# Three more projections of a two-layer transformer block as seven block products each

## What is computed

```python
# even layer; h, hc are the normed tokens and context, (256, 1024) each
aq, ak, av, nq, nk, nv = split_cols(h @ w_in, (512,) * 6)        # the same for hc
# odd layer
cq, ckv, kr, rq, rk, rv, rg = split_cols(h @ w_in, (256, 128, 32, 256, 256, 512, 512))
r = rms_norm(retention(rq, rk, rv, ...)) * silu(rg)              # rg of the 256 tokens alone
```

## Time and profile before

| | before |
|---|---|
| median of 3 runs | 1845.21 us (1843.87 to 1847.04) |
| the profiled execution | 1846.67 us |
| its span, first to last instruction | 1844.9 us |
| TensorE matmul busy | 1601.1 us (87%) |
| VectorE busy | 700.1 us (38%) |
| ScalarE busy | 337.3 us (18%) |
| moved | 538.32 MB, mean 292 GB/s |
| mean granted TensorE clock | 0.955 |

### The profile page before, as it was taken

How to read it: one execution, slowest core, us unless ns; L and a number is a source line. 1 busy time by engine, 2 the same in 40 slices (tenths; PEclk the granted TensorE clock), 3 DMA queues, 4 the chain that set the end, 5 groups by cost and what they waited for, 6 DMA issues and landing times. The chain is left out here.

```text
span 1844.9 us, 23772 instructions
## 1 busy us (share of the span) xinstructions
PE 1601.1 (87%) x9876; PEld 860.6 (47%) x9876; DVE 700.1 (38%) x1473; ACT 337.3 (18%) x836; POOL 37.8 (2%) x40
## 2 busy tenths in 40 slices
PE   6999999999999999999989889899998665665665
PEld 3844684447884654333333233374655332232322
DVE  1267838766755853323223131330643111020202
ACT  2222227412002842000000000122431000000000
POOL 0000200000000000000000000000000000000000
PEclk9999999999999999999999999999999888788877
DMA  9312238874345032899999999921359999999997
GB/s 384 139 46 91 92 137 368 373 303 171 137 183 214 18 137 90 354 428 428 427 429 427 428 427 428 385 98 71 138 227 377 426 428 427 426 428 427 426 428 300
DMA packets 39966, 538.32 MB, mean 292 GB/s; under 512 B 4394, under 2 KB 4906, under 8 KB 6964
## 3 DMA queue, kind: packets, MB, share of 16 engines
q1 hardware_dynamic: 39860, 536.81, 70.2%
HBM read 535.74 MB, written 1.05 MB: 291 GB/s over the span
## 5 line engine op out<-in xcount | busy, mean ns | idle before, releaser
L675 PE MATMUL bank<-mem 128*32 128x256 f32 (+13 forms) x9112 | 1490.9, 473 | 221.3 <-DMA mem<-in_moe 145.5
L675 PEld LDWEIGHTS bank<-mem 128*32 128x32 f32 (+4 forms) x9112 | 774.6, 146 | 872.0 <-issue 583.4
L2637 ACT ACTIVATE mem<-bank 128x512 f32<-128x512 f32 (+6 forms) x262 | 127.6, 503 | 1027.7 <-PE bank L675 908.0
L2384 DVE TENSOR_TENSOR mem<-mem,bank 128x512 f32<-128x512 f32 (+1 forms) x32 | 17.8, 557 | 459.0 <-PE bank L675 459.0
L685 PE MATMUL bank<-mem 128*128 128x128 f32 x736 | 116.8, 285 | 14.2 <-ACT mem L2637 3.4
L2402 DVE TENSOR_TENSOR mem<-bank,mem 32x512 f32<-32x512 f32 (+1 forms) x120 | 66.6, 555 | 159.2 <-PE bank L675 158.0
L685 PEld LDWEIGHTS bank<-mem 128*128 128x128 f32 x736 | 81.2, 142 | 93.0 <-issue 45.4
L1872 DVE SCALAR_TENSOR_TENSOR mem<-mem 128x256 f32<-128x256 f32 x160 | 86.8, 543 | 10.4 <-issue 0.9
L1732 DVE SCALAR_TENSOR_TENSOR mem<-mem 128x512 f32<-128x512 f32 x76 | 57.1, 751 | 23.3 <-DMA mem<-in_w_ada 15.2
L2991 POOL TENSOR_TENSOR mem<-mem 128x1 f32<-128x1 f32 (+5 forms) x20 | 16.1, 805 | 1433.1 <-DVE mem L1683 1433.1
L2355 DVE TENSOR_TENSOR mem<-bank,mem 128x256 f32<-128x256 f32 x48 | 20.2, 421 | 48.6 <-PE bank L685 48.6
(11 more groups left out here) (217 smaller groups left out, 599.2 us busy)
## 6 DMA issues: line engine op xcount, KB each, us to landing
mem<-in_moe SPq DMA_DIRECT2D x188, 2048.0 KB, 39.7
mem<-in_ada_w SPq DMA_DIRECT2D x24, 2048.0 KB, 10.3
mem<-in_w_in SPq DMA_DIRECT2D x10, 2048.0 KB, 8.4
mem<-in_w_ada SPq DMA_DIRECT2D x6, 2048.0 KB, 14.7
mem<-in_even_w_in SPq DMA_DIRECT2D x6, 2048.0 KB, 7.5
mem<-in_w_out SPq DMA_DIRECT2D x4, 2048.0 KB, 12.4
mem<-in_moe SPq DMA_DIRECT2D x8, 1024.0 KB, 23.4
mem<-in_odd_w_in SPq DMA_DIRECT2D x3, 2048.0 KB, 8.3
```

Source lines behind the costliest of these rows:

```text
L675: return nc.tensor.matmul(o, lhsT, rhs, start=start, stop=stop, skip_group_check=True)
L2637: took(name, S.activation(o, i, func))
```

## The change

`SEVEN` gets three more entries, and `seven(n)` takes `nv`, `rv` and `rg`. For `rg`, whose output is 256 tokens, a product is 4 matmuls (one half bank), with token sums of its own. The neighbourhood scores' and the diff scores' first units stand between the last products of `nv`. `ada_sum(28)` moves into `seven(4)`, `ada_sum(29)` behind it. On VectorE `ada_part(29)` is cut in three and stands between the block reads and the first units' softmax work. The expert slot at `TAIL`, where the token sums lie, is loaded after `nv12` instead of `nk12`, and in layer 1 after `rv12`. The list of loads is otherwise as it was. The diff, cut to its core:

```diff
-        SEVEN = [("k", 1, k_fm, v_tok), ("v", 2, v_tok, nq_fm), ("nq", 3, nq_fm, nk_fm), ("nk", 4, nk_fm, nv_tok)]
+        SEVEN = [("k", "even1", k_fm, v_tok), ("v", "even2", v_tok, nq_fm), ("nq", "even3", nq_fm, nk_fm), ("nk", "even4", nk_fm, nv_tok), ("nv", "even5", nv_tok, None),
+                 ("rv", "odd_rv", rv_tok, mv_tok), ("rg", "odd_rg", rg_tok, mv_tok)]
...
+        prods = [[r.take(TOK), r.take(TOK)]] * 5 + [[mk[:, 0, :], mk[:, 1, :]], [mk[:, 2, 0:SEQ], mk[:, 3, 0:SEQ]]]
...
@@ TensorE, seven(n)
                 product(t21, w_block(w, 0, 1), ts[:, 2]).then_inc(part_ready, 1)
+                if name == "nv":
+                    wait_took(pe, "nk11")
+                    wait_took(pe, "nk12")
+                    unit_scores(0)
                 pe.wait_ge(first_read, n + 1)
-                B.close(t11, product(t11, w_block(w, 1, 0), h_block(1, 0), False))
-                if name != "k":
+                B.close(t11, product(t11, w_block(w, 1, 0), h(1, 0), False))
+                if 0 < n < 5:
                     ada_sum(24 + n)
                 pe.wait_ge(part_read, 2 * n + 2)
...
+                if name == "nv":
+                    unit_scores(1)
                 pe.wait_ge(w_last, n + 1)
...
@@ TensorE, in front of the attention loop
-            w = use("even5")
-            for j in range(4):
-                t = B.open(f"nv{j}", "act")
-                B.close(t, token_major(t.ps[:, :], w, j, 0, 512))
-                if j == 0:
-                    ada_sum(28)
-                    wait_took(pe, "nk11")
-                    wait_took(pe, "nk12")
-                if j == 1:
-                    unit_scores(0)
-                    unit_scores(1)
-                if j == 2:
-                    ada_sum(29)
-                    unit_scores(2)
-                    unit_scores(3)
-            done_with("even5")
-            wait_took(pe, "nv3")
+            seven(4)
+            ada_sum(29)
+            unit_scores(2)
+            unit_scores(3)
+            wait_took(pe, "nv11")
+            wait_took(pe, "nv12")
             router_bias(0)
...
@@ TensorE, odd layer: the loops over rv0 to rv3 and rg0, rg1
+            seven(5)
+            seven(6)
             router_bias_rows(1)
...
@@ VectorE, even layer
             blocks_22(3)
+            sum_1(4)
             ada_part(28, 0, 2)
             sum_4(3)
+            sum_2(4)
             ada_taken(27)
             ada_part(28, 2, 4)
             block_21(3)
             ada_part(28, 4, 5)
             block_12(3)
+            sum_3(4)
             ada_part(28, 5, 8)
-            ada_gate(28)
-            ada_part(29)
-            settle()
-            for n in (4, 5):
-                gains(n)
+            blocks_22(4)
...
+            ada_part(29, 0, 2)
+            sum_4(4)
+            ada_gate(28)
             d_max(0)
-            for k in range(1, AHEAD):
+            block_21(4)
+            ada_part(29, 2, 4)
+            unit_max(1)
+            block_12(4)
+            combine(0)
+            ada_part(29, 4, 8)
+            ada_gate(29)
+            settle()
+            for n in (4, 5):
+                gains(n)
+            for k in range(2, AHEAD):
                 unit_max(k)
-                if k == 1:
-                    combine(0)
-                    ada_gate(29)
             n_scale(0)
             router_scale(0)
...
@@ VectorE, odd layer, behind the tables of ret_d
+            settle()
+            token_sums(("4a", "4b"))
+            sum_1(5)
+            sum_2(5)
+            sum_3(5)
+            four_sums(tok_sum_g, h_rows)
+            blocks_22(5)
+            sum_1(6)
+            sum_4(5)
+            settle()
+            sum_2(6)
+            block_21(5)
+            sum_3(6)
+            block_12(5)
+            blocks_22(6)
+            sum_4(6)
+            block_21(6)
+            block_12(6)
             router_bias_rows(1)
...
@@ ScalarE
-            for j in range(4):
-                take(f"nv{j}", nv_tok[:, j, :], arrive(act, f"nv{j}")[:, :])
...
+            first_copy(4)
+            unit_exp(0)
+            first_out(4)
+            for k in range(1, AHEAD):
+                unit_exp(k)
...
-            for j in range(2):
-                take(f"rg{j}", rg_tok[:, j, :], arrive(act, f"rg{j}")[:, :], ACT.Silu)
+            first_copy(5)
+            first_out(5)
+            first_copy(6)
+            first_out(6)
+            wait_took(act, "rg21")
+            S.activation(rg_tok[:, 0, SEQ:TOK], rg_tok[:, 0, SEQ:TOK], ACT.Silu).then_inc(gate_act, 1)
+            wait_took(act, "rg12")
+            S.activation(rg_tok[:, 1, :], rg_tok[:, 1, :], ACT.Silu).then_inc(gate_act, 1)
...
@@ SyncE, load_experts: what the first load of a slot waits for
-    (layer 0) 11: "nk12"
+    (layer 0) 11: "nv12"      (layer 1) 11: "rv12"
```

More of the change, by code:

```diff
@@ L1108, in seven @@
             def seven(n):
-                name, i = SEVEN[n][:2]
-                w = use(f"even{i}")
+                name, source = SEVEN[n][:2]
+                w = use(source)
+                h, ts = (h_rows, tok_sum_g) if name == "rg" else (h_block, tok_sum)
                 def product(t, a, b, start=True):
-                    for q in range(2):
+                    for q in range(1 if name == "rg" else 2):
                         for kt in range(4):
                             o, c = t.ps[:, SEQ * q:SEQ * q + SEQ], slice(P * q, P * q + P)
-                            if name == "v":
+                            if name in ("v", "nv", "rv", "rg"):
                                 last = mm(o, b[:, kt, c], a[:, kt, :], start and q == kt == 0, kt == 3)
@@ L1123, in seven @@
                 t11 = B.open(f"{name}11", "act")
-                product(t11, w_block(w, 0, 0), h_block(0, 0)).then_inc(part_ready, 1)
+                product(t11, w_block(w, 0, 0), h(0, 0)).then_inc(part_ready, 1)
                 if name == "k":
@@ L1987, in chunk_of @@
             def chunk_of(n):
-                return chunk_view(f"even{SEVEN[n][1]}")
+                return chunk_view(SEVEN[n][1])
             def sum_1(n):
-                name = f"even{SEVEN[n][1]}"
+                name = SEVEN[n][1]
                 dve.wait_ge(filled[place[name]], 16 * fill_no[name])
@@ L2025, in blocks_22 @@
                 o = out_block(n, 1, 1)
-                ps = arrive(dve, f"{name}x")
+                first, two = prod_view(n, 0), prod_view(n, 1)
+                arrive(dve, f"{name}x")
                 dve.wait_ge(first_read, n + 1)
-                took(f"{name}x", V.scalar_tensor_tensor(out=two_prods, in0=ps[:, :], scalar=scale_of(n), in1=first_prod, op0=ALU.mult, op1=ALU.add))
+                took(f"{name}x", V.scalar_tensor_tensor(out=two, in0=bank_view(n, tiles[f"{name}x"].ps), scalar=scale_of(n), in1=first, op0=ALU.mult, op1=ALU.add))
                 settle()
-                V.scalar_tensor_tensor(out=o, in0=two_of(tiles[f"{name}12"].ps[:, :]), scalar=scale_of(n), in1=two_of(two_prods), op0=ALU.mult, op1=ALU.add).then_inc(part_read, 1)
+                V.scalar_tensor_tensor(out=o, in0=bank_view(n, tiles[f"{name}12"].ps), scalar=scale_of(n), in1=two, op0=ALU.mult, op1=ALU.add).then_inc(part_read, 1)
                 settle()
                 dve.wait_ge(part_ready, 3 * n + 3)
-                V.scalar_tensor_tensor(out=o, in0=two_of(tiles[f"{name}21"].ps[:, :]), scalar=scale_of(n), in1=o, op0=ALU.mult, op1=ALU.add).then_inc(part_read, 1)
+                V.scalar_tensor_tensor(out=o, in0=bank_view(n, tiles[f"{name}21"].ps), scalar=scale_of(n), in1=o, op0=ALU.mult, op1=ALU.add).then_inc(part_read, 1)
             def block_21(n):
@@ L2038, in block_21 @@
                 o = two_of(rope_raw[1]) if name == "k" else out_block(n, 1, 0)
-                took(f"{name}21", V.scalar_tensor_tensor(out=o, in0=two_of(ps[:, :]), scalar=scale_of(n), in1=two_of(two_prods), op0=ALU.mult, op1=ALU.add))
+                took(f"{name}21", V.scalar_tensor_tensor(out=o, in0=bank_view(n, ps), scalar=scale_of(n), in1=prod_view(n, 1), op0=ALU.mult, op1=ALU.add))
             def block_12(n):
@@ L2043, in block_12 @@
                 ps = arrive(dve, f"{name}12")
-                took(f"{name}12", V.scalar_tensor_tensor(out=out_block(n, 0, 1), in0=two_of(ps[:, :]), scalar=scale_of(n), in1=two_of(two_prods), op0=ALU.mult, op1=ALU.add))
+                took(f"{name}12", V.scalar_tensor_tensor(out=out_block(n, 0, 1), in0=bank_view(n, ps), scalar=scale_of(n), in1=prod_view(n, 1), op0=ALU.mult, op1=ALU.add))
             def turn_query(m):
@@ L2766, in _, with first_copy @@
                 took(f"q{m}", S.activation(rope_raw[m % 2][:, 0:SEQ], ps[:, 0:SEQ], ACT.Copy, scale=-NA_SCALE))
-            for n, (name, _, _, _) in enumerate(SEVEN):
+            def first_copy(n):
+                name = SEVEN[n][0]
                 scale = -NA_SCALE if name == "nq" else 1.0
@@ L2776, in _ @@
                 o = two_of(rope_raw[0]) if name == "k" else out_block(n, 0, 0)
```

(7 more changed lines are left out.)

107 lines of the change are left out of this document (53 added, 54 removed).

## The result

The changed kernel takes 1856.64 us (median of four runs, 1856.15 to 1857.23), the kernel before beside it 1846.03. These medians lie 10.6 us apart (0.57%). 1855.9 was predicted, with +10.7. The profiled execution took 1857.23 us (span 1855.4), against 1846.67 (span 1844.9).

The account below looks back on a forecast made before the run. Expert-weight DMA sets the time once flowing, so serial projection stages ahead, bound by TensorE, shift the end one for one. Even stage +13.5, clock +2.0, odd stage -4.8 make +10.7 us: 1855.9 us, range 1852.5 to 1859.5.

Parts of the forecast that it names:

- Part 1: TensorE's products: 3.3 us less for neighbourhood values, 3.3 for retention values, 1.7 for the gate; 8.3 us less work in all.
- Part 2: Odd stage, retention values and gate: TensorE ends 5.0 us earlier, exp table load 4.8 earlier, VectorE's sums in time; -4.8 us.
- Parts 3 and 4: Even stage: last product at 584.3; step 29, slabs, then router's weights delay router bias from 590.7 to 604.2: +13.5 us.
- Part 5: TensorE's clock after idling from 584 to 604: first attention units begin at half clock; +2 us, at most 3.4.
- The sum: Whole kernel: +13.5 even stage, +2.0 clock, -4.8 odd stage, giving +10.7 us.
- one-for-one rule: Attention stages ahead of the expert loads: whatever a stage gains or loses moves the transfers and the end equally.
- (a): Router load before even attention: not held up by two slabs, lands 6.4 us after issue; +7.5, 1849.9 us; chance 0.09.
- (c): Attention loop: clock at half for longer, or half-clock stretches before the experts fall worse; 1861 us; chance 0.10.
- (b): Even stage: no wait for router's weights, VectorE's own work fits; gain 3.3 + 4.8, 1837.1 us; chance 0.07.

Follow-up runs that it names:

- the even half alone: The changed kernel with the odd layer's retention values and gate put back as in the kernel before: 1861.15 us, ratio 1.0083 to the kernel before.

## Why the prediction was right

**Part 1** holds as a count of work. It is a gain of time only where nothing stands behind it: 4.94 of the odd layer's 5.0 us up to the gate's end, 1.7 of the even layer's 3.3 at best.

**Part 2** was right in its mechanism and a little high. TensorE ends the gate 4.94 us earlier, where 5.0 was said, so VectorE's sums were not in the way. At the exp table load 4.8 was booked and 4.45 measured (the lag goes from 14.27 to 1295.45 - 1285.63 = 9.82), since VectorE's last combining and the Silu behind it put the table load 1.11 us behind the gate's end instead of 0.62: 0.49 more, where 0.24 was taken. Some more of it went again: TensorE's wait for ScalarE in the next step, 1.41 us in the earlier trace rows, is 1.89 in the changed kernel, and the lag goes from 9.3 to 10.5 by the end.

**Parts 3 and 4** were right in each link and their order, with errors of up to a microsecond that nearly cancel. The changed execution lay 0.7 us behind before the change begins (SP's issues of the same transfers up to 537 us all lie that much later). The last product ended at 586.06, where 584.3 was said: 0.7 of that from upstream, 1.0 from a sum that was too short. The first four products took what was said (13.83 us between VectorE's reads at 558.64 and 572.47). Most of the 1.0 lies at the three places where scores or ada_sum(28) stand between block products: there the weight loads of the products lie 1.39, 0.89 and 1.39 us apart, 0.13 of which is their usual distance, and 0.96, 0.55 and 0.95 were booked. Step 29 ended at 591.6 against 590.1. From the first slab to the router's arrival it took 12.6 us (604.3 - 591.66), not 13.3. TensorE entered the router bias at 605.38, against 604.2.

**Part 5**: the loop's head is 1.74 us longer than before, +2 was said. The expected sign in the records is there: 0.50 granted from 590 to 610. What the price rests on is the length of the loop head, 11.24 us against 9.50; it is 11.22 in the second trace of the changed kernel and in that of the even half alone. The run with matmuls in the gap recovers a third of the difference, and the clock fell in it as well, so the price has no run that isolates it.

**The sum.** At the first steady row the lag is 16.4 us, 15.7 without upstream, against 15.5 predicted. Two terms were not in the sum: the upstream 0.7, and 1.6 us given back between the end of the even attention and the start of the retention values, where the transfers set the time. The prediction said that a loss passes through that stretch one for one. In this trace nine tenths of it did; in the second trace of the changed kernel (the last run) the lag grows over the same stretch instead, from 14.7 to 15.8 us, and is 11.7 at the end of the span. So the 1.6 doesn't repeat, and single traces can't test the one-for-one rule more closely than that. With 0.5 lost from the lag in the even attention and the odd stage's later loss of 1.2, these terms nearly cancel, so 10.5 against 10.7 is closer than the working deserves: that part is luck.

**The rivals.** (a) falls: the router's weights land 11.5 us after their issue, not 6.4, and in 2.1 when they go first. (c) falls too: the clock is back from 610 on, and the half-clock stretch at the end of the attention cost no more than the one before (over ten microseconds 0.66 both times). (b) was judged by the wrong point. I wrote that it hangs on whether the router's weights are there by 586.3. With them there at 581.5 the kernel was no faster than before (0.9996), since VectorE's own list came next; and even with that mended the ratio is 0.9971, where 1837.1 would be 0.9956. The sentence that failed is "VectorE's own work fits": it fits by its total, not by its order. It changed nothing in the forecast, since the transfer was longer.

## What to carry to other kernels

When work is cut into pieces behind another engine's last result, follow everything that hangs on its last piece, the queue of loads included: here 5.6 us of wait on TensorE became 16, and 7.7 of that came from a small load that stood behind two large ones. A small load that the next stage needs goes ahead of large ones in its queue. Before trusting a repaired wait, ask what the waiting instruction's producer has in front of it in its own order: the wait for the transfer hid a wait for VectorE's list.

## What the runs showed of the hardware

128 KB on SP's queue land in 2.1 to 2.2 us when issued ahead of two 2 MB slabs. Issued behind their first one by 6.9 us they take 6.4, by 3.6 us 9.1, by 0.8 to 1.1 us 11.5 to 12.8, and once 14.1 (the odd layer's load in the run with matmuls in the gap). They come when both slabs are through: in the changed kernel the slabs of 592 land 7.4 and 12.0 us after their issue, the second at 604.0, and the router's weights at 604.3; in the kernel before 587.9 and 588.3. The Trainium skill ("DMA: Bandwidth & Descriptors") has both rules: that descriptors are consumed in ring order ("Queues, rings and completion order"), and, for transfers issued by GpSimd, about 2 us fixed ("Anatomy of one DMA — SWDGE (gpsimd) path"). The traces agree with each in its place, here for loads that SyncE issues.

The clock fell behind a gap that was filled with matmuls (1.00 up to 605, 0.66 from 605 to 610, with only 1.34 and 1.37 us idle around them), which I had not expected. In the changed kernel, with the gap empty, it was at 0.50 for 20 us and back within 5 us of TensorE's return.
